# A two-layer transformer kernel: the order of small steps changed at three places between the large matmuls

## What is computed

```python
# layer 1
xn = rmsnorm(h)
q_a, k_a, v_a, q_b, f_b, i_b, og_b, g_a, g_b = split(xn @ w_in)
y_a = moba_attention(q_a, k_a, v_a) @ w_br_attn      # 16 heads, causal softmax
y_b = hgrn2(q_b, f_b, i_b, og_b) @ w_br_hgrn         # gated linear recurrence
h = h + (sigmoid(g_a) * y_a + sigmoid(g_b) * y_b) @ w_out
h = h + cross_attention(rmsnorm(h), rmsnorm(mem))    # mem: 256 x 1024, keys = mem @ wkv_x
h = h + swiglu(rmsnorm(h))
# layer 2, twice: half a swiglu, a mixer, half a swiglu
#   mixer 0: NSA, compressed keys (an MLP over blocks of the keys, then a norm),
#            selected blocks and a window, added under gates
#   mixer 1: differential attention, 8 heads with two score maps each:
#            P = softmax(S1) - lambda * softmax(S2);  o = rmsnorm_head(P @ v)
```

## Time and profile before

| | |
|---|---|
| three runs | 1679.9, 1692.11, 1686.15 us (median 1686.15) |
| the profiled execution | 1679.9 us, of which the span of its instructions is 1678.1 us |
| mean granted clock of TensorE | 0.997 of full speed |
| DMA | 284 MB, mean 169 GB/s |

### The profile page before, as it was taken

How to read it: one execution, slowest core, us unless ns; L and a number is a source line. 1 busy time by engine, 2 the same in 40 slices (tenths; PEclk the granted TensorE clock), 3 DMA queues, 4 the chain that set the end, 5 groups by cost and what they waited for, 6 DMA issues and landing times.

```text
span 1678.1 us, 32155 instructions
## 1 busy us (share of the span) xinstructions
PE 1647.0 (98%) x14060; PEld 1598.3 (95%) x14060; DVE 1078.4 (64%) x1331; ACT 919.8 (55%) x1248; POOL 159.3 (9%) x63
## 2 busy tenths in 40 slices
PE   7999999999999999999999899999999999999999
PEld 7999989999999999999998699999999998799999
DVE  6888868674665567765578856655655557665553
ACT  6966778445444455444487844444443447754432
POOL 0000000000022101220000002210122000012210
PEclk9999999999999999999999999999999999999999
DMA  7554443544355465545542235546554564245544
GB/s 267 185 178 161 142 151 128 199 176 151 129 200 185 157 206 203 185 162 183 199 148 101 102 127 199 178 156 200 202 198 162 173 222 149 103 147 187 186 156 129
DMA packets 44636, 284.12 MB, mean 169 GB/s; under 512 B 4944, under 2 KB 6608, under 8 KB 17744
## 3 DMA queue, kind: packets, MB, share of 16 engines
q1 hardware_dynamic: 44352, 281.99, 48.9%
q10 hardware_dynamic: 144, 0.08, 0.0%
HBM read 281.00 MB, written 1.05 MB: 168 GB/s over the span
## 4 chain that ended last, share of the span: by engine, by line
PE 84%; DVE 7%; ACT 6%; issue 2%; DMA 1%; DVEq 0%; ACTq 0%
PE bank L509 83%; ACT WH L1150 2%; DVE WL L1735 2%; PE bank L658 1%; ACT SB L1273 1%; DVE HT L1791 1%; DVE STAT L1878 0%; ACT XR L1157 0%; DVE XM L1743 0%; ACT FB L1174 0%; ACT XM L1157 0%; DVE FB L1761 0%; DMA RAW<-in_nsa_w_out 0%; DMA PAR<-in_par 0%; DVE SB L1875 0%
## 5 line engine op out<-in xcount | busy, mean ns | idle before, releaser
L1735 DVE TENSOR_TENSOR WL<-RAW,WH 128x2048 fp32r<-128x2048 f32 (+1 forms) x282 | 590.6, 2096 | 288.7 <-ACT WH L1150 288.1
L509 PE MATMUL bank<-XR,WH 128*128 128x256 f32 x3648 | 649.1, 281 | 11.2 <-DVE WL L1920 10.6
L1150 ACT ACTIVATE WH<-RAW 128x2048 fp32r<-128x2048 f32 (+1 forms) x282 | 493.3, 1752 | 230.3 <-PE bank L509 224.2
L509 PEld LDWEIGHTS bank<-XR,WH 128*128 128x128 f32 x3648 | 559.3, 189 | 15.5 <-DVE WL L1920 10.6
L509 PE MATMUL bank<-XR,WL 128*128 128x256 f32 x1824 | 510.8, 280 | 0.0
L509 PEld LDWEIGHTS bank<-XR,WL 128*128 128x128 f32 x1824 | 344.2, 189 | 0.0
L509 PE MATMUL bank<-XF,WH 128*128 128x256 f32 x1760 | 310.7, 280 | 0.0
L509 PE MATMUL bank<-XM,WH 128*128 128x256 f32 x1664 | 296.1, 281 | 3.2 <-DVE XM L1743 1.8
L509 PEld LDWEIGHTS bank<-XF,WH 128*128 128x128 f32 x1760 | 269.0, 188 | 0.0
L509 PEld LDWEIGHTS bank<-XM,WH 128*128 128x128 f32 x1664 | 254.9, 188 | 4.8 <-DVE XM L1743 2.7
L509 PE MATMUL bank<-XF,WL 128*128 128x256 f32 x880 | 246.4, 280 | 0.0
(11 more groups left out here) (278 smaller groups left out, 1592.5 us busy)
## 6 DMA issues: line engine op xcount, KB each, us to landing
RAW<-in_f1i SPq DMA_DIRECT2D x44, 1024.0 KB, 4.8
RAW<-in_f2i SPq DMA_DIRECT2D x44, 1024.0 KB, 4.9
RAW<-in_w_in SPq DMA_DIRECT2D x35, 1024.0 KB, 4.9
RAW<-in_w_ffn_in SPq DMA_DIRECT2D x22, 1024.0 KB, 4.8
RAW<-in_f1o SPq DMA_DIRECT2D x32, 704.0 KB, 4.1
RAW<-in_f2o SPq DMA_DIRECT2D x32, 704.0 KB, 4.1
RAW<-in_diff_w_in SPq DMA_DIRECT2D x12, 1024.0 KB, 4.9
RAW<-in_w_ffn_out SPq DMA_DIRECT2D x16, 704.0 KB, 4.1
```

The source lines that it names most:

```text
L509: return e.matmul(o, l, r, start=start, stop=stop)
L1150: e.activation(split_at(u, cols)[0], RAW[:, u % NRAW, 0:cols], ACT.Copy).then_inc(hi_done.tick(u), 1)
L1735: e.tensor_tensor(lo, RAW[:, u % NRAW, 0:cols], hi.bitcast(f32), sub).then_inc(lo_done.tick(u), 1)
```

## The change

Nothing is added or taken away: the same instructions are issued, in another order, and one result goes to another bank.

In the branch stage ACT squares the memory in j = 0 instead of j = 1, and DVE adds the squares up in j = 1 instead of j = 3. DVE also loses a special place for moba(6) and moba(7): they stood ahead of the weight split in j = 2 and 3, and now stand at the end of the step like all others. In the nsa stage unit 5 writes to bank 0 instead of bank 3, and the steps of the compressed keys come one p earlier on PE, ACT and DVE. In the diff stage transposing and weighing lag the scores by one step more (3 and 4 instead of 2 and 3), the loop has twelve steps, and within a step PE transposes ahead of the scores, ACT takes the exponentials ahead of the scaling, and DVE mixes ahead of its weight split; the norm and the projection pieces follow one step later.

```diff
@@ tensor, nsa stage
                 if p == 3:
-                    nsa_unit(5, ("cmp", 1), "third")
+                    nsa_unit(5, ("cmp", 1))
...
-                if p == 9:
-                    compressed_keys()
                 if p in (7, 9):
                     compress(1, p // 9, "one")
                 if p == 8:
                     nsa_unit(3, ("q", 3), "third")
+                    compressed_keys()
                 if p == 9:
+                    compressed_key_sum()
                     nsa_sum(("q", 3))
-                if p == 10:
-                    compressed_key_sum()
@@ tensor, diff stage
-            for p in range(11):
+            for p in range(12):
+                if 0 <= p - 3 < 8:
+                    turn_mixed(p - 3)
                 if p < 8:
                     score_pair("diff", p, ...)
-                if p == 8:
-                    diff_out(1, 0, 2)
-                if 0 <= p - 2 < 8:
-                    turn_mixed(p - 2)
...
-                if p == 7:
-                    diff_out(0, 0, 2)
-                if 0 <= p - 3:
-                    h = p - 3
+                if 0 <= p - 4:
+                    h = p - 4
...
-                if p in (9, 10):
-                    diff_out(p - 9, 2, 4)
-                if p in (5, 7, 9):
-                    od_sum((p - 5) // 2)
+                if p in (8, 9):
+                    diff_out(p - 8, 0, 2)
+                if p in (10, 11):
+                    diff_out(p - 10, 2, 4)
+                if p in (6, 8, 10):
+                    od_sum((p - 6) // 2)
@@ scalar, branch stage
-                    if j == 1:
+                    if j == 0:
                         q.wait_ge(parts, ("ob", 7))
                         e.activation(SQM, MEM, ACT.Square)...
@@ scalar, nsa stage: copy and square of the keys from p == 9 to p == 8, root from p == 10 to p == 9
@@ scalar, diff stage
-            for p in range(11):
+            for p in range(12):
+                for n in {0: (2, 8), ...}.get(p, ()):
+                    asked(("diff_w_in", n))
                 if p in (1, 2, 4, 5):
                     diff_square({1: 2, 2: 6, 4: 3, 5: 7}[p])
-                for n in {0: (2, 8), ...}.get(p, ()):
-                    asked(("diff_w_in", n))
+                if p in (6, 8, 10):
+                    od_square((p - 6) // 2)
+                if 0 <= p - 3 < 8:
+                    turn_over("diff", 2 * p - 5)
...
-                if p in (5, 7, 9):
-                    od_square((p - 5) // 2)
-                if 0 <= p - 2 < 8:
-                    turn_over("diff", 2 * p - 3)
-                if p in (6, 8, 10):
-                    n = (p - 6) // 2
+                if p in (7, 9, 11):
+                    n = (p - 7) // 2
                     rows_root(("od", n), RS_O, ("od", n - 1) if n else None)
...
+                if p < 8:
+                    score_pair("diff", p)
                 if 0 <= p - 1 < 8:
                     scale_second(p - 1)
-                if p < 8:
-                    score_pair("diff", p)
...
-                if p in (6, 8, 10):
-                    n = (p - 6) // 2
+                if p in (7, 9, 11):
+                    n = (p - 7) // 2
                     q.wait_ge(normed, ("od", n))
                     high_part(("od", n), half(OD, n), XO, n * 512, 512)
@@ vector, branch stage
             for j in range(8):
-                if j in (2, 3):
-                    moba(j + 4)
                 asked(("w_br_hgrn", j) if j < 4 else ("wkv_x", j - 4))
                 if j < 4:
                     for k in (2 * j, 2 * j + 1):
                         norm_lo("mem", k, tiles(MEM, 256)[:, k, :])
+                    if j == 1:
+                        q.wait_ge(sqd, "mem")
+                        q.wait_ge(hgrn_o, 3)
+                        add_up(SQM, "mem")
                 if 1 <= j <= 4:
                     branch_b(j - 1)
...
-                if j not in (2, 3):
-                    for i in MOBA_STEPS.get(36 + j, ()):
-                        moba(i)
-                if j == 3:
-                    q.wait_ge(sqd, "mem")
-                    q.wait_ge(hgrn_o, 3)
-                    add_up(SQM, "mem")
+                for i in MOBA_STEPS.get(36 + j, ()):
+                    moba(i)
@@ vector, nsa stage: the product of the keys (L2336) from the start of p == 11 to the end of p == 10
@@ vector, diff stage
-            for p in range(11):
-                if p in (7, 9):
-                    diff_out_lo((p - 7) // 2)
+            for p in range(12):
+                if p in (8, 10):
+                    diff_out_lo((p - 8) // 2)
...
                 if 0 <= p - 1 < 8:
                     settle_diff(p - 1)
-                if p in (6, 8, 10):
-                    diff_out((p - 6) // 2)
+                if 0 <= p - 2 < 8:
+                    mix(p - 2)
+                if p in (7, 9, 11):
+                    diff_out((p - 7) // 2)
...
                 if p == 7:
-                    mix(6)
                     asked(("diff_w_out", 0))
...
-                if 0 <= p - 1 < 8 and p != 7:
-                    mix(p - 1)
```

28 lines of the change are left out of this document (14 added, 14 removed).

## The result

The changed kernel takes 1706.49 us (median of 7 runs, 1697.78 to 1711.54), the kernel before in the same comparison 1687.14 (7 runs, 1679.9 to 1693.24). The ratio is 1.0102, 95% interval 1.0079 to 1.0126: 17.2 us longer (13.3 to 21.3). The two medians lie 19.4 apart, which is within that. The kernel is slower; whether by more or by less than 1%, the runs don't decide. The profiled execution took 1708.82 us (span 1707.0), 28.9 more than the profiled one of before.

The account below looks back on a forecast made before the run. PE, 98% busy, was taken as the bound. Terms 5.9 + 1.6 + 2.2 + 2.5 + 4.2 = 16.4 us gave 1696.3 on the profiled execution, 1702.6 on the median; forecast 1700 us, range 1687 to 1713.

Parts of the forecast that it names:

- part 3: Diff stage: longer lag of transposing and weighing brings new waits of 7.1 us against 4.6 before; cost 2.5 us.
- the clock: PE's granted clock drops behind the new long waits in branch stage (2.4 us) and diff stage (1.8 us); together 4.2 us.
- Part 1: Memory norm and moba: DVE reaches moba(6)'s scores later, so PE waits at the transposes of pair 5; cost 5.9 us.
- Part 2: Nsa stage: unit 2 waits for unit 5's bank, 1.6 us; compressed keys' wait is handed on by DVE, 2.2 us.
- Rival 2: The clock falls in all three places, for the long stretch each: 21.8 us, 1706 us; chance 0.15.
- Rivals 1, 3 and 4: 1: clock holds, 1696 us, 0.12; 3: longer diff lag works, 1691, 0.11; 4: not slower, waits go, 1679, 0.06.

Follow-up runs that it names:

- part 1 alone: The kernel before with only the memory norm and moba edits of the change (squares taken and added up earlier, moba units later); ratio 1.0048 (1.0030 to 1.0065).
- moba last alone: The kernel before with only DVE's order changed: moba units of j = 2 and 3 at the end of their step; ratio 1.0038 (1.0014 to 1.0061).

## Why the prediction was right, and where it was not

The forecast was 1700 us, within 1687 to 1713; measured 1706.49. Its sum of 16.4 us stands against 17.2 (13.3 to 21.3). That it is this near is partly luck: part 3 was 1.3 us too small and the clock 1.3 too large, and the two errors cancel. Term by term:

- **Part 1, 5.9 us: right.** 5.8 without a drop of the clock. The place was half right: PE stands 4.3 us at the scores of moba(7), two operations ahead of the transposes of pair 5, and only 0.2 at these. The prediction overlooked that the score banks are freed by the same late DVE tile. It costs nothing more, since both wait for one chain: the transposes start at 284.50, 5.84 later than before.
- **Part 2, 1.6 + 2.2 = 3.8 us: right as a sum,** 3.7 in the changed kernel and 3.8 alone. Both are estimates, worked out with the line for the clock, which holds to 0.7. The waits are 1.58 and 2.65 as worked out, none is left at the compressed scores, and the gain there was handed on to the transposes behind. The split between the two edits is not confirmed: alone they read 2.0 and 3.1 without the late transfer.
- **Part 3, 2.5 us: too small, 3.8.** The step on the new waits held: 2.68 + 2.69 = 5.4 for 5.6, 0.84 for 0.9, 0.47 + 0.19 for 0.6, together 6.9 for 7.1. So did that on the old: the 0.7 at the first score pair, the 1.2 and the 2.7 gone or shrunk. What failed is the step from waits to cost, "new waits 7.1 against 4.6". The difference of the table is 2.3 (2.5 with the waits under 0.2 us that it leaves out), that of the stage 3.8. A wait in the table begins at the modelled end of the matmul ahead. In a full queue the weighing gives way to the next row after 0.66 us (1453.89 to 1454.55 in the kernel before); ahead of a stop it is counted with 0.92. So a stop costs about a quarter of a microsecond beyond its bracket. The changed stage has it four times (2.68, 2.69 and the new ones of 0.19 and 0.47) where the kernel before has it at 2.71. Behind the first stop of the changed kernel the transposes also hold the weighing up for 0.57 us (1479.67 to 1480.24), where they take 0.33 in a full queue (1456.83 to 1457.16); behind the stop of the kernel before they took 0.36, so that isn't a price of every stop. The prediction put all of this at nothing. Together it is about 0.9 of the missing 1.3 us; the rest was not traced.
- **The clock, 4.2 us: right in place, too large in size, 2.9.** It fell at the two places named, for 6.83 us each and not 5.1, and cost 2.0 in the diff stage (1.8 predicted) and 0.9 in the branch stage (6.6 less 5.8; 1.8 in part 1 alone; 2.4 predicted). What the price of 0.47 per us left out is that much of such a stretch falls into the wait itself, where a slow clock costs nothing: it begins at 279.70 and PE stands until 281.16. The granted clock of all the runs agrees with the places. At two levels, time at 0.50 is twice (1 - mean clock) times the span: on average 41.4 us in 40 runs of the changed kernel and 23.7 in 91 of the kernel before. The 17.7 between them (standard error 1.2) agree with the three new stretches of the profiled execution, 6.83 + 3.41 + 6.83 = 17.1.
- **Rival 2** (a drop in all three places, 1706) came nearest by its number, but only because of the base: its 21.8 us lie outside the measured 13.3 to 21.3. By its mechanism it is half true: there is a drop of 3.4 us at the compressed keys, but nothing shows that the long one behind it is the change's. Rivals 1, 3 and 4 fall: the clock fell, the old waits of the diff stage gave way to longer ones, and PE had to wait in j = 3.
- **The base.** The prediction compared with a profiled execution that was lucky: 1679.9 us with 10.9 us at 0.50, where 23.7 is the mean. It saw that this one was the fastest of three and went nearer to the median, to 1700; the sum on the median, 1702.6, would have been nearer still.

Of the 28.9 us between the two profiled executions, 6.6 + 3.7 + 5.7 = 16.0 are these terms, and 7.4 is the nsa stage's clock. Another 3.9 us lie in the dense units behind the nsa stage (the 339 matmuls for 343). The rest is 2.1 in the dense units between branch and nsa stage, 1.6 in the time around the longer stretch at 0.50 near 832 (6.83 us for the 3.4 of the earlier trace rows), and -2.1 in the last stage, where it was the kernel before that had 339 matmuls in 40 us (1560 to 1600) and the changed one 343 (1590 to 1630). The parts alone add up to 0.48 + 0.36 + 0.42 = 1.26%, the whole is 1.02% (0.79 to 1.26): they add, within what was measured.

The Trainium skill (TensorE: Matmul & The Clock Gate, "HAM oscillation — how this bites in real kernels") prices a throttled stretch at half of its length. The runs show less: 0.36 in the nsa stage, where PE also has waits, 2.0 of 6.83 (0.29) behind the waits of the diff stage. Only where PE computes without a gap do the rows come near half, 0.47. The same page of the Trainium skill ("What's actually happening") puts the ramp at the start of a kernel at under 1% of a typical span; the prediction carried that over to the drops within this one. Here the two priced drops make 2.9 us of some 17: under 1% of the span indeed, but a sixth of the effect.

## What to carry to other kernels

Follow the engine that hands over, not only the one that waits: PE's stalls at three places were the sum of what had been put ahead of one tile in DVE's or ACT's order, and that sum, read off the timeline of before, gave the waits to 0.2 us. To get from waits to time, add a quarter of a microsecond or more per stop of PE to what the table shows, and price a clock drop only for the part in which the engine computes. Before using one profile as the base, look at its granted clock among the clocks of the other runs, and compare stage by stage rather than by the whole time. A stage length is of one execution too: look whether a transfer landed late in it before giving the difference to the edit.

## What the runs showed of the hardware that was not expected

- The clock falls at other places and for other lengths from one execution to the next, though the program is the same up to there: from 6.8 to 30.7 us in the nsa stage with its order unchanged. Over 91 runs of the kernel before, the time follows it: from a fit, 0.38 us per us at 0.50 (correlation 0.8).
- A wait of 2.8 us brought the clock down in one stage (moba last alone), one of 2.7 us did not in another, and in the nsa stage it fell with waits of 1.3 us and less before it, among narrow matmuls. What decides was not settled.
- Dead matmuls in a wait kept the clock up at both places with long waits, and the diff stage gained 2.0 us from 40 matmuls whose result nobody reads. In the nsa stage the clock fell 6 us behind them.
- One weight transfer of 1 MB, issued at the same place, landed about 1 us later in four of fourteen executions.
- At a granted clock of 1.00 dense matmuls ran at two rates, 343 and 339 in 40 us, each for long parts of an execution. Their cause stays open.
